# A two-block transformer kernel: branch weight loads moved ahead of gate reloads, the short branch reloaded early, convolution taps and the norm's mean pulled into the pairs, the first pair reordered

## The reference, cut to what matters

```python
h = rmsnorm(x, g_mix[i])
z = jnp.einsum("bsd,dn->bsn", h, w_in[i])
a_val, a_gt = z[..., :o1], z[..., o1:o2]
sc_b, sc_c, sc_v = z[..., o2:o3], z[..., o3:o4], z[..., o4:o5]
gate_logits = z[..., o5:] + b_gate[i]
g_a = jax.nn.sigmoid(gate_logits[..., :D_MODEL])
g_b = jax.nn.sigmoid(gate_logits[..., D_MODEL:])

a = a_val * jax.nn.sigmoid(a_gt)
a = causal_dwconv(a, conv_a_w[i]) + conv_a_b[i]          # 31 taps
a = jax.nn.silu(layernorm(a, ln_a_g[i], ln_a_b[i]))
y_a = jnp.einsum("bsc,cd->bsd", a, w_a_out[i])

s = sc_b * causal_dwconv(sc_c * sc_v, conv_b_w[i])       # 3 taps
y_b = jnp.einsum("bsc,cd->bsd", s, w_b_out[i])

x = x + jnp.einsum("bsd,de->bse", g_a * y_a + g_b * y_b, w_o[i])
...
```

## Time and profile before

| what | us |
|---|---|
| median of three runs | 1977.53 (1976.48 to 1982.11) |
| the profiled execution, its own time | 1980.39 |
| span of the profiled execution, first to last instruction | 1978.6 |
| PE busy in the span | 1916.8 |

### The profile page before, as it was taken

One profiled execution on the slowest core, in us unless ns is written; L12 is line 12 of the kernel. 1 busy time (PEld: TensorE's weight loads), 2 busy tenths in 40 slices (PEclk: granted clock), 3 DMA queues, 4 the chain that ended last, 5 costly groups with the idle time before them and its releaser, 6 DMA issues.

```text
span 1978.6 us, 24375 instructions
## 1 busy us (share of the span) xinstructions
PE 1916.8 (97%) x9137; PEld 1590.9 (80%) x9137; DVE 1358.6 (69%) x1419; ACT 679.6 (34%) x932; POOL 859.3 (43%) x612
## 2 busy tenths in 40 slices
PE   7999999997999999999999999999999999999998
PEld 6788888776888888888888788878787878888877
DVE  6778999754447898988988785654724746666521
ACT  5433344331225333333341200343321245565511
POOL 5755655423324556555557455422133513112321
PEclk9999999998999999999999999999999999999999
DMA  4112233426111232232355435111131310000043
GB/s 165 43 50 79 85 107 107 181 101 195 35 52 44 86 96 84 75 95 64 96 175 198 148 113 175 43 32 43 33 128 53 90 34 1 12 12 1 1 139 95
DMA packets 191306, 166.41 MB, mean 84 GB/s; under 512 B 11171, under 2 KB 168816, under 8 KB 191216
## 3 DMA queue, kind: packets, MB, share of 16 engines
q1 hardware_dynamic: 189936, 162.82, 26.0%
q10 hardware_dynamic: 1280, 2.35, 0.4%
HBM read 134.73 MB, written 30.41 MB: 83 GB/s over the span
## 4 chain that ended last, share of the span: by engine, by line
PE 82%; DVE 9%; issue 3%; POOL 2%; ACT 2%; DMA 1%; SPq 0%; ACTq 0%; POOLq 0%; DVEq 0%
PE ps L870 35%; PE ps L1151 19%; PE ps L1018 16%; PE ps L1384 2%; PE ps L1417 1%; PE ps L1419 1%; PE ps L1418 1%; PE ps L1395 1%; PE ps L1398 1%; PE ps L1401 1%; PE ps L1392 1%; POOL wlo L757 1%; PE ps L1404 1%; POOL h_raw L766 1%; DVE win_a L2696 1%
## 5 line engine op out<-in xcount | busy, mean ns | idle before, releaser
L870 PE MATMUL ps<-xb_hi,whi 128*128 128x512 f32 x768 | 255.8, 399 | 25.5 <-POOL wlo L757 15.1
L752 POOL TENSOR_TENSOR small<-ones 128x1 f32<-128x1 f32 x82 | 26.2, 319 | 584.0 <-PE ps L870 431.5
L870 PE MATMUL ps<-xb_lo,whi 128*128 128x512 f32 x768 | 251.1, 393 | 0.0
L870 PE MATMUL ps<-xb_hi,wlo 128*128 128x512 f32 x768 | 250.7, 392 | 0.0
L757 POOL TENSOR_TENSOR wlo<-raw,whi 128x1024 fp32r<-128x1024 f32 (+1 forms) x79 | 212.0, 2683 | 6.6
L870 PEld LDWEIGHTS ps<-xb_hi,whi 128*128 128x128 f32 x768 | 144.5, 190 | 62.5 <-issue 21.4
L795 POOL TENSOR_TENSOR wlo<-w_sums,whi 128x512 fp32r<-128x512 f32 x80 | 137.9, 1743 | 82.3 <-ACT whi L1788 82.3
L870 PEld LDWEIGHTS ps<-xb_lo,whi 128*128 128x128 f32 x768 | 146.0, 190 | 31.0 <-issue 0.5
L870 PEld LDWEIGHTS ps<-xb_hi,wlo 128*128 128x128 f32 x768 | 145.8, 190 | 31.1
L2135 DVE SCALAR_TENSOR_TENSOR ps<-glu_pad,tab,ps 128x1024 f32<-128x1024 f32 x116 | 149.3, 1287 | 3.0
L870 PE MATMUL ps<-xa_hi,whi 128*128 128x512 f32 x448 | 143.6, 396 | 1.4 <-DVE xa_lo L2433 0.6
(11 more groups left out here) (431 smaller groups left out, 4611.4 us busy)
## 6 DMA issues: line engine op xcount, KB each, us to landing
t<-in_w_mod SPq DMA_DIRECT2D x48, 256.0 KB, 2.9
f_scratch<-t SPq DMA_DIRECT2D x22, 512.0 KB, 2.7
raw<-in_w_down SPq DMA_DIRECT2D x22, 512.0 KB, 4.1
raw<-in_w_up SPq DMA_DIRECT2D x40, 256.0 KB, 3.8
w_raw<-in_w_up SPq DMA_DIRECT2D x40, 256.0 KB, 3.8
raw<-in_w_in SPq DMA_DIRECT2D x18, 512.0 KB, 3.9
raw<-in_w_in SPq DMA_DIRECT2D x36, 256.0 KB, 3.9
w_in_raw<-in_w_in SPq DMA_DIRECT2D x32, 256.0 KB, 3.7
```

What stands on the lines that cost most here:

```text
L752: nc.gpsimd.tensor_tensor(small[:, 106 + slab.slot:107 + slab.slot], ones[:, 0:1], ones[:, 0:1], ALU.mult)
L870: ins = mm(dst[j], w, r[j], start=first and f, stop=last and l)
```

## The change

1. **Order of the first products.** `WIN_AT` starts with (0,1) (0,2) (0,5) (1,1) (0,6) (1,2) (0,7) (0,4) (0,3), then (1,6) (1,5) (1,7) (2,1) (1,4) (1,3), and goes on as before from pair 2. The four sums of pair 0 are made by DVE into the free tiles `pair_first` and `pair_second`, ahead of everything else; POOL no longer makes s3 of pair 0. The combinations are interleaved otherwise on DVE and ACT.
2. **Taps.** `TAP_ENDS` gets a third place in the "cv" pairs, one tap before the short taps and one behind. Pairs 0 to 8 take 65 taps in place of 50, pairs 9 to 16 take 59 in place of 74, and pair 16 none.
3. **The norm.** The sum over the four tiles is made in pairs 13, 14 and 15. The two all-ones products for the mean stand behind (16,7), two centrings behind `win_c22` of pair 16, two behind `win_c12`.
4. **The short branch.** Its tiles come back into `glu_pad`, whose inputs are used up: three at pair 14, the last at pair 16; ACT and DVE split them within pair 16.
5. **The first job of each branch** runs all matmuls with the high part of the input first, then those with the low part (`branch_first_product`).
6. **SP's order.** Slabs stand ahead of gate loads; the loads of `x` follow later in two groups of eight.
7. **DVE's order in the branch stage.** The multiplications `mix_b` are interleaved otherwise with the norm; column sums stand behind job 2 and the broadcast behind job 3 (before: 4 and 5).

```diff
-for _p in range(NWP):
-    for _k in ((1,) if _p == 0 else ()) + (2, 6, 5, 7):
+for _pk in ((0, 1), (0, 2), (0, 5), (1, 1), (0, 6), (1, 2), (0, 7), (0, 4), (0, 3)):
+    WIN_AT[_pk] = len(WIN_AT)
+for _p in range(1, NWP):
+    for _k in (6, 5, 7) if _p == 1 else (2, 6, 5, 7):
         WIN_AT[_p, _k] = len(WIN_AT)
...
-for _p, _n in enumerate(((0, 0), (5, 3), (5, 3), (2, 3), (2, 3), (4, 3), (2, 3), (2, 3), (4, 3),
-                         (6, 4), (5, 4), (6, 4), (5, 4), (6, 4), (5, 4), (5, 4), (5, 3))):
+for _p, _n in enumerate(((0, 2, 0), (5, 3, 0), (5, 3, 0), (5, 3, 2), (2, 3, 2), (4, 3, 0), (4, 3, 2), (2, 3, 2), (4, 3, 0),
+                         (5, 4, 0), (5, 4, 0), (5, 4, 0), (5, 4, 0), (5, 4, 0), (5, 3, 0), (4, 2, 0), (0, 0, 0))):
...
+            if p == 14:
+                sp.wait_ge(sem("conv_tap"), 3 * TAPS_A)
+                sp.wait_ge(sem("pair_out1"), stored(5))
+                sp.wait_ge(sem("pair_out0"), stored(8))
+                sp.dma_start(gpad[:, 0:3, 0:S], sdram[0:3].rearrange("t p n -> p t n")).then_inc(sem("consts_in"), 16)
+            if p == NWP - 1:
+                sp.wait_ge(sem("conv_tap"), 4 * TAPS_A)
+                sp.dma_start(gpad[:, 3, 0:S], sdram[3]).then_inc(sem("xn_in2"), 16)
...
         gate_load(1)
...
+        out_slab(2)
         win_store(NWP - 1)
         sp.wait_ge(sem("pair_out0"), stored(16))
         gate_load(2)
         gate_load(3)
...
+        out_slab(3)
+        for n in range(4, 7):
+            gate_load(2 * n - 4)
+            gate_load(2 * n - 3)
+            out_slab(n)
...
+        for p, k in WIN_AT:
+            win_product(p, k)
+            if (p, k) == (NWP - 1, 7):
+                pe.wait_ge(sem("ln_v"), 3)
+                for a in (0, H):
+                    last = mm(conv_ps[:, a:a + H], ones[:, :], T[1][:, a:a + H], start=True, stop=True)
+                last.then_inc(sem("ln_pe"), 1)
...
+        def branch_first_product(job, slab, place, hi_ready, lo_ready):
+
+            s = slab.slot
+            for low in (False, True):
+                for c in range(2):
+                    k0, c0 = place[c]
+                    for k in range(KC):
+                        pe.wait_ge(*(lo_ready if low else hi_ready)(c, k))
...
+        win_sums(0, (1, 3, 4))
         dve.wait_ge(sem("h_raw"), 5)
         dve.wait_ge(sem("x_hi"), 8)
-        for n in range(4):
-            token_sub(n)
-        win_sums(0, (1,))
-        token_low2(0, 3)
-        token_low2(1, 3)
+        token_sub(0)
+        token_sub(1)
+        token_sub(2)
+        token_low2(0)
```

More of the change, by code:

```diff
@@ L552, in sync_program, with out_slab, x_columns_in @@
         gate_load(1)
+        def out_slab(n):
+            name, w = (("mix_b", A["w_b_out"][0]), ("mix_a", A["w_a_out"][0]))[n // 4]
+            slabk(Lin(SLABS[name] + n % 4), w, KC, (n % 4) * 2 * P, 2 * P)
+        def x_columns_in(m):
+            c0 = H if m >= 4 else 0
+            for u, to in enumerate((xcolh, hraw)):
+                sp.dma_start(to[:, m, c0:c0 + H].rearrange("p (t f) -> p t f", f=P),
+                             A["x"][0, u * H:(u + 1) * H, m * P:(m + 1) * P].rearrange("(t p) f -> p t f", p=P)
+                             ).then_inc(sem(f"load_in{m // 4}"), 16)
+        out_slab(2)
         win_store(NWP - 1)
@@ L556, in sync_program @@
         gate_load(3)
[L557 to L569, removed]
-                c0 = H if m >= 4 else 0
-                for u, to in enumerate((xcolh, hraw)):
-                    sp.dma_start(to[:, m, c0:c0 + H].rearrange("p (t f) -> p t f", f=P),
-                                 A["x"][0, u * H:(u + 1) * H, m * P:(m + 1) * P].rearrange("(t p) f -> p t f", p=P)
-                                 ).then_inc(sem(f"load_in{m // 4}"), 16)
+        out_slab(3)
[3 more added lines that the diff above has]
+            out_slab(n)
+        gate_load(10)
+        gate_load(11)
+        sp.wait_ge(job_done, JOBS["mix_a"])
+        for m in range(4):
+            x_columns_in(m)
+        out_slab(7)
+        gate_load(12)
+        gate_load(13)
+        for m in range(4, 8):
+            x_columns_in(m)
+        gate_load(14)
+        gate_load(15)
         with sp.Fori(0, KD // 2) as q:
@@ L770, in win_third_sum @@
             win_raw_in(pool, p)
[L771 to L776 removed]
+            nc.gpsimd.tensor_tensor(win_sum(p, 2), win_raw(p, 0), win_raw(p, 2), ALU.subtract).then_inc(sem("win_sum3"), 1)
         for g in range(WIN_PRODUCTS):
@@ L1020, in win_product, with branch_product @@
             last.then_inc(sem("win_done"), 1)
-        win_product(0, 1)
-        for p in range(NWP):
-            for k in (2, 6, 5, 7):
-                win_product(p, k)
-            if p + 1 < NWP:
-                win_product(p + 1, 1)
-            for k in (4, 3):
-                win_product(p, k)
-        def branch_product(job, slab, m, place, new_slab, ready=None):
+        for p, k in WIN_AT:
[5 more added lines that the diff above has]
+                last.then_inc(sem("ln_pe"), 1)
+        def branch_product(job, slab, m, place):
             s = slab.slot
@@ L1044, in branch_product @@
                                           [XBh[:, k0 + k, q]], [XBl[:, k0 + k, q]], k == 0, k == KC - 1,
-                                          1 if new_slab and (c, k) == (0, 0) else None)
+                                          1 if m % 2 == 0 and (c, k) == (0, 0) else None)
+            last.then_inc(job_done, 1)
+        def branch_first_product(job, slab, place, hi_ready, lo_ready):
[5 more added lines that the diff above has]
+                        pe.wait_ge(*(lo_ready if low else hi_ready)(c, k))
+                        w = slice(k * 2 * P, k * 2 * P + P)
+                        o, q = pair(job, H * c, H * (c + 1)), slice(c0, c0 + H)
+                        if low:
+                            last = mm(o, whi[:, s, w], XBl[:, k0 + k, q], start=False, stop=k == KC - 1, skip_group_check=True)
+                        else:
+                            first = mm(o, whi[:, s, w], XBh[:, k0 + k, q], start=k == 0, stop=False, skip_group_check=True)
+                            if (c, k) == (0, 0):
+                                first.then_inc(slab_begun, 1)
+                            mm(o, wlo[:, s, w], XBh[:, k0 + k, q], start=False, stop=False, skip_group_check=True)
             last.then_inc(job_done, 1)
```

173 lines of the change are left out of this document (95 added, 78 removed).

## The result

| | before | changed |
|---|---|---|
| median of 4 executions each | 1979.82 us | 1959.29 us |
| lowest and highest | 1976.48, 1983.8 | 1956.1, 1959.75 |
| profiled execution | 1980.39 us | 1959.75 us (span 1958.0) |

The ratio is 0.9892, with a 95% interval of 0.9868 to 0.9916: faster by about 1.1%. The forecast was 1944 us with a range of 1938 to 1956, so the direction was right and the gain too large: 20.6 us between the two profiled executions in place of 33.7.

What follows compares the result with a forecast made beforehand. PE, busy 97% of the span, bounds the kernel, so gains come only from its waits and slow stretches. 28.7 (branch stage) + 5.4 (first pair) - 0.4 (taps) = 33.7 us, giving a median of 1944 us, range 1938 to 1956.

Steps and rivals of the forecast that it cites:

- The slabs: Branch stage: slabs load some 16 us before POOL wants them, against 4.6 us to land, so none is late.
- The end of the pairs and the branch stage: From the end of (16,7) to the end of job 16: 98.2 us against 126.93, 28.7 us gained, bounds 22 and 34.
- The copy wait: Pair 16, ACT's copy of (16,7) behind the short branch's second high part: 0.6 us added, ends 0 and 2.
- Column sums and broadcast: The norm's small products in the branch stage, taken at 1.7 us each, between 0 and 3.
- The first pair: Start of the pairs: (0,1) at 48.0, nine products over at 74.6 against 80.0, gain 5.4 us, bounds 7.5 and 1.5.
- Rival B: First pair gives nothing: waits at (0,5) and (0,6) each exceed 3 us, the clock falls; 1949 us, chance 0.12.
- The taps: Pairs 0 to 8 take 15 more taps, mostly filling idle time; `win_c22` 0.5 us late in pair 8; loss 0.4 us.

Runs made afterwards that it cites:

- the second profile: The changed kernel run again with nothing edited: median 1958.59 us, ratio 0.9886; its profiled execution had a span of 1954.6 us.
- the kernel with both moves: Changed kernel with the third sum of pair 1 behind the split for (0,3) and tile 3's reload first in pair 16: 1951.19 us, ratio 0.9845.

## Why the prediction was right and wrong

**The slabs: right.** No slab was late, the three waits are gone, and SP's waits on `mixed` stay without a PE wait behind them, as forecast.

**The end of the pairs and the branch stage: right in mechanism, 4.8 us too large (28.7 against 23.9).** Four sizes were off. The copy wait was set at 0.6 us from "if tile 3 has landed by 369.5 us (issued near 365.5, 4.6 us to land)". It was issued at 367.00, since SP stood at the first slab's wait ahead of it, and took 6.2 us; (16,4) started 3.29 us behind (16,7) in place of 2.3. The late split of the first slab, 1.0 us, wasn't in the sum. Column sums and broadcast cost about what was taken, but PE lost 0.7 to DVE ahead of them. The slow stretch behind them cost 1.7 and doesn't come in each execution. That adds up to 4.4. With tile 3 issued 5 us earlier the stage took 98.6 us against the forecast's 98.2 (to a mark 0.16 us later). That close a match is partly luck: (16,4) then started 1.0 us less behind (16,7) than forecast, while the 0.7 ahead of the column sums stayed.

**The first pair: wrong, -1.0 (by the second profile -0.4) against +5.4.** PE started (0,1) at 48.05 as forecast, DVE's subtractions started at 42.33 (42 forecast), and the waits at (0,5) and (0,4) were 0.95 and 0.84 (1.1 and 0.9; the terms that lead to 54.5 add up to 54.3). The step that failed is "(0,6) needs a subtraction and a low part more, 60.0, where PE is at 59.9". It followed DVE alone, and DVE was on time: its low part for (0,6) was over at about 60.0. POOL's queue was never written down: five instructions between 51.3 and 67.7, of 3.3 us each beside DVE's, with the third sum of pair 1 ahead of (0,6). It gives 64.5 for (0,6), a wait of 3.54 us, and a granted clock of 0.77 behind it. The earlier trace rows already showed 3.41 against 1.28 us for such an instruction, but it was used only to move DVE's start. Rival B had the outcome (waits over 3 us, slow clock, nothing gained) and the same contention, but for both (0,5) and (0,6) and on the wrong queue. With that one instruction moved the pair gives 3.1 us; what is left of the 5.4 is four waits of 0.25 to 0.29 us for POOL. Each costs about 0.55 with the slower starts around it, since POOL's 3.3 us a split exceed PE's 2.72 a product.

**The taps: the loss of 0.4 us didn't come.** In the changed kernel `win_c22` was over at 169.9 us in pair 5 and at 227.1 in pair 8, some 0.8 us ahead of its product (the forecast's times for it, 169.8 and 226.9, and 1.0), and PE had no wait over 0.25 us from 75.5 to 374.8. That isn't only because PE was 1.0 us late: with the third sum moved PE ran 4.1 us earlier, with no wait in the pairs either. The step also counted wrongly: it gives pairs 6 and 7 four taps more, where the table gives them six (nine in place of five, seven in place of five). And its terms for pair 5 (1.3 + 1.3 - 0.66 - 0.66) leave 1.3 us, not 1.6. So the idle time that the taps fill was underrated by more than the 0.4 us shows.

**Behind job 16: 2.3 us more, which no step spoke of.** The twelve profiled executions took 1478.0 to 1481.1 us there, and the changed kernel alone 1480.3 and 1479.0. The kernel before has one of the two shortest, equal to the one with only the third sum moved. So the 2.3 us are within what executions differ by, and no cause in the change is shown. Part of the difference is in which places the granted clock fell.

## What to carry to other kernels

Where two engines contend, write down the queue of each one instruction by instruction at the slowed duration, not only of the one that seems busiest, and ask of every instruction in it whether it must stand there: one sum, wanted much later, cost 3.4 to 4.1 us. When instructions take turns, neither their number nor their length is free: cutting one engine's work into pieces hands turns to the other, which helps only if the one that is cut can wait. Who gets the first turn can hang on a tenth of a microsecond, so look at what an edit adds beside its purpose: here a wait. A transfer ordered behind a wait for something else is as late as that wait, however early its own data are ready.

## What the runs showed of the hardware

- A POOL instruction of 128x512 with two SBUF inputs took 1.29 us alone, 1.71 beside DVE instructions of 128x512 and 3.3 beside those of 128x2048. DVE's 128x2048 took 2.28 us with its turn free and 3.3 to 3.4 when it had to give one up first.
- The granted clock can be near the lower of its two levels (1.2 GHz of 2.4) while PE reads as busy without a pause: 0.57 in 1270 to 1274 us of the changed kernel, 0.73 in its second execution. What PE did before isn't the same as in other stretches: it stood 0.58 us and then made 16 products of one column each. The first line is the changed kernel's window, the second that of the kernel with both moves, whose program is 8 us earlier there:

```profile
1270.00:1274.00 4.00, 4.00 (x13) 3.17 (x13) 3.50 (x4) 0.21 (x1) 0.00 (x0) 0.57 0.00 0
```
```profile
1262.00:1266.00 4.00, 4.00 (x13) 3.13 (x12) 3.76 (x5) 0.14 (x1) 0.00 (x0) 0.57 0.00 0
```

  Such a stretch costs 0.43 x 4 = 1.7 us. Behind 1200 us two to four slices of 10 us had a clock below 0.97 in each execution, not at the same places in each kernel. Why the clock falls behind these small products at one time and not at another stays open.
